# gMLP mixer of a macaron decoder step: squares of v added by transfers, mixing spread over three u chunks, first output product behind the fifth

## The chip, the cores and the metric

The kernel runs on one core of one Trainium2 chip. The metric is device time in microseconds (us), the median over runs of the same program. Everything is float32. Each large product is made of three TensorE products: operands are split into a high part (`_hi`, type float32r) and a rest (`_lo`), and hi·hi, lo·hi and hi·lo are added in PSUM.

## The reference

One step of a decoder trunk for 512 prompt tokens and 8 sample tokens (520 columns, TOK) with width 1024: per layer half a SwiGLU, a mixer, half a SwiGLU. The change lies in the mixer of layer 0, a gated MLP of inner width 2048:

```
def gmlp_mixer(h, w_in, b_in, v_gain, w_s, b_s, w_out):
    z = jax.nn.gelu(h @ w_in + b_in)
    u, v = z[..., :D_GMLP], z[..., D_GMLP:]
    v = rms_norm(v, v_gain)
    s = chunk_spatial_mix(v, w_s, b_s)   # per group g: (128x128 lower triangle of w_s[g]) @ v in blocks of 128 tokens, + b_s
    return (u * s) @ w_out, v
```

v needs its norm over all 2048 channels before anything can be mixed; u and the mixing go group by group (8 groups of 256 channels); for sample tokens the mixing is one factor and one bias per group.

## The kernel before, in words

Activations lie transposed: channels on the 128 partitions, the 520 tokens in the free dimension, `HALF` = 260 columns.

**Chunks.** `w_in` is worked through in 16 chunks of 256 columns: eight for v (v0 to v7 here), then eight for u (u0 to u7), then `w_out` in two output products of four chunks. A chunk of `w_in` is one `fast_chunk`: a Strassen-like scheme with seven blocks instead of eight (j = 0 to 6), each of 4 x 3 matmuls of 260 columns, so 84 matmuls. The blocks need sums of weight quarters (`sums_w`), and those take five engines:

- SP (SyncE) starts four loads per chunk (`load_fast`, L612, L616), two chunks ahead, when a `raw` slot is free.
- POOL (GpSimd) starts two transfers that add inside SBUF: `add_inner` (L3152, `sums_w<-raw`) when the loads have landed, `add_outer` (L3157, `raw<-raw`) when the first add has landed.
- DVE (VectorE) makes two more sums (`sums_second` L2207, `sums_last` L2214), the `_lo` rests of the weights (L2197), and takes the results out of PSUM (L2340, L2347, L2359, L2361, L2365: low0, high1, high0, both highs, low1).
- ACT (ScalarE) rounds weights to `w_hi` (L1492, L1496, L1501, L1516, L1518), copies three PSUM snapshots per chunk (L1573, L1579, L1589) and does Square and Gelu.
- PE (TensorE) runs the blocks (L842). Before block 6 it waits until DVE has taken high1 (L2347) out of the bank.

Every engine runs its own list in order and waits only on semaphores. Hooks (`between`, `steps`, `ready`, `mixing`, `own`, `held`, `behind`, `after`) put other work at set places of a chunk.

**Squares of v.** After each v chunk ACT squares its two channel tiles into `square` (L1477). POOL adds them into `square_sum` by two tensor instructions per chunk (`add_squares`, L3147; the first one is the copy L3144). The last pair is added during u0. Then PE sums over partitions (`rms_v`, L1025 to L1028, hook 5 of u0), ACT takes the root, DVE the reciprocal (`sample_gains`), and SP may load the biases `bs_all` into the tile `square` (L679; it waits for the finished sum, and SP's loads for u2 stand behind it in SP's list).

**Mixing.** For group g: PE transposes v (`turn_v`, L1041, L1042), ACT scales it into `v_tok` (L1920), PE multiplies by the mixing matrix (`mix`, L1053), DVE adds gain and bias into `tmp_mul` (L2772), POOL multiplies it with gelu(u) in `tmp_act` (L3222, two instructions of 128x520 per group), ACT copies to `hv`, DVE makes `h_lo` (L2784). Before, all of that for g stands in chunk u-g and the start of the next one. The first output product (`down`, L792) stands behind u3, the second behind u7.

## Time and profile before

| | |
|---|---|
| median of 3 runs | 2080.99 us (2080.2 to 2087.7) |
| the profiled execution's own time | 2089.98 us |
| its span in the profile | 2088.1 us |
| PE busy | 2042.7 us (98%) |
| DVE busy | 1677.0 us (80%) |
| ACT, POOL busy | 1170.7 us (56%), 372.2 us (18%) |
| granted TensorE clock | 0.998 of full |

The v chunks stand at about 374 to 466 us of the span, u0 to u3 at 466 to 526, the first output product at 528 to 574, u4 to u7 at 574 to 630, the second product from 632. The profile gives for every instruction its start and duration, and for idle time in front of it the instruction that ended it.

### The profile page before, as it was taken

How to read it: one execution, taken by the hardware profiler on the slowest of the kernel's cores; microseconds unless marked ns; L12 is line 12 of the kernel's file. 1: busy time of each engine (PE TensorE's matmuls, PEld its weight loads, DVE VectorE, ACT ScalarE, POOL GpSimd, SP SyncE). 2: the span in 40 equal slices, each digit the busy share in tenths (PEclk: the TensorE clock that was granted, in tenths of full speed). 3: DMA queues.
4: the chain of work that ended last, by engine and by line, in shares of the span. 5: the costliest groups of instructions: out<-in, count | busy, mean ns of one | idle time of the engine just before them, and what ended most of it. 6: DMA issues, size and time to landing. Idle time of an engine off the chain costs nothing.

```text
span 2088.1 us, 44481 instructions
## 1 busy us (share of the span) xinstructions
PE 2042.7 (98%) x16512; PEld 1972.9 (94%) x16512; DVE 1677.0 (80%) x2836; ACT 1170.7 (56%) x2101; POOL 372.2 (18%) x413
## 2 busy tenths in 40 slices
PE   9999999989999999999999999999999999999998
PEld 8999999988999999999999999998768889999998
DVE  6779887887477998998899998679665468989997
ACT  5446565666264655655665655445564346656555
POOL 0011111333131111110111111111122121111111
PEclk9999999999999999999999999999999999999999
DMA  5467775664445777775777777451322126777775
GB/s 160 123 162 179 181 184 149 148 152 122 112 112 128 175 179 176 181 186 151 168 177 181 178 186 181 129 138 28 96 72 81 61 61 158 179 184 176 187 181 128
DMA packets 385039, 307.52 MB, mean 147 GB/s; under 512 B 22951, under 2 KB 346836, under 8 KB 384628
## 3 DMA queue, kind: packets, MB, share of 16 engines
q1 hardware_dynamic: 343418, 231.03, 37.0%
q0 software_dynamic: 41152, 74.09, 21.9%
q8 instruction: 93, 1.52, 0.3%
q10 hardware_dynamic: 314, 0.37, 0.1%
q14 instruction: 62, 0.51, 0.1%
HBM read 228.76 MB, written 2.66 MB: 111 GB/s over the span
## 4 chain that ended last, share of the span: by engine, by line
PE 79%; DVE 6%; DMA 6%; issue 4%; ACT 2%; POOL 1%; SPq 1%; DVEq 0%; ACTq 0%; POOLq 0%
PE side L842 29%; PE main L842 20%; PE main L792 16%; DMA raw<-raw 2%; PE side L1389 2%; DVE w_lo L2197 2%; PE main L1151 2%; DMA sums_w<-raw 1%; DMA raw<-in_ffn_w_down 1%; PE main L1319 1%; PE side L1359 1%; POOL tmp_act L3222 1%; DMA raw<-in_ffn_w_gate 1%; PE side L1241 1%; PE main L1221 1%
## 5 line engine op out<-in xcount | busy, mean ns | idle before, releaser
L842 PE MATMUL side<-xw_hi,w_hi 128*128 128x260 f32 x1600 | 455.0, 284 | 20.1 <-DVE v L2347 9.2
L842 PE MATMUL side<-xw_hi,w_lo 128*128 128x260 f32 x1600 | 453.5, 283 | 0.0
L842 PE MATMUL side<-xw_lo,w_hi 128*128 128x260 f32 x1600 | 452.4, 283 | 0.0
L2197 DVE TENSOR_TENSOR w_lo<-raw,w_hi 128x512 fp32r<-128x512 f32 (+2 forms) x540 | 382.8, 709 | 71.0 <-ACT w_hi L1518 22.2
L842 PE MATMUL main<-xw_hi,w_hi 128*128 128x260 f32 x1200 | 341.5, 285 | 0.0
L842 PE MATMUL main<-xw_lo,w_hi 128*128 128x260 f32 x1200 | 338.9, 282 | 0.0
L842 PE MATMUL main<-xw_hi,w_lo 128*128 128x260 f32 x1200 | 338.7, 282 | 0.0
L842 PEld LDWEIGHTS side<-xw_hi,w_hi 128*128 128x128 f32 x1600 | 301.4, 188 | 25.6 <-DVE w_lo L2197 8.5
L842 PEld LDWEIGHTS side<-xw_hi,w_lo 128*128 128x128 f32 x1600 | 301.3, 188 | 0.0
L842 PEld LDWEIGHTS side<-xw_lo,w_hi 128*128 128x128 f32 x1600 | 301.0, 188 | 0.0
L2197 DVE TENSOR_TENSOR w_lo<-sums_w,w_hi 128x1024 fp32r<-128x1024 f32 (+2 forms) x264 | 250.3, 948 | 3.2 <-ACT w_hi L1501 3.2
L3152 POOL DMA_DIRECT2D sums_w<-raw x132 | 116.0, 879 | 756.0 <-DMA raw<-in_ffn_w_gate 321.9
L1516 ACT ACTIVATE w_hi<-raw 128x512 fp32r<-128x512 f32 (+1 forms) x132 | 83.2, 630 | 264.0 <-PE main L842 143.3
L842 PEld LDWEIGHTS main<-xw_hi,w_hi 128*128 128x128 f32 x1200 | 226.5, 189 | 0.2
L842 PEld LDWEIGHTS main<-xw_lo,w_hi 128*128 128x128 f32 x1200 | 226.2, 189 | 0.0
L842 PEld LDWEIGHTS main<-xw_hi,w_lo 128*128 128x128 f32 x1200 | 226.2, 189 | 0.0
L3157 POOL DMA_DIRECT2D raw<-raw x132 | 113.9, 863 | 399.6 <-DMA sums_w<-raw 399.6
L792 PE MATMUL main<-h_lo,w_hi 128*128 128x260 f32 x896 | 179.8, 282 | 0.0
L1496 ACT ACTIVATE w_hi<-raw 128x512 fp32r<-128x512 f32 (+1 forms) x264 | 164.2, 622 | 3.8 <-PE main L842 2.1
L1501 ACT ACTIVATE w_hi<-sums_w 128x1024 fp32r<-128x1024 f32 (+1 forms) x132 | 139.5, 1057 | 40.2 <-DVE sums_w L2207 38.2
L842 PE MATMUL side<-ht_hi,w_hi 128*128 128x260 f32 x496 | 140.9, 284 | 2.2 <-DVE tmp_in L2347 1.6
L842 PE MATMUL side<-ht_lo,w_hi 128*128 128x260 f32 x496 | 139.7, 282 | 0.0
(485 smaller groups left out, 4895.2 us busy)
## 6 DMA issues: line engine op xcount, KB each, us to landing
sums_w<-raw POOLq DMA_DIRECT2D x128, 256.0 KB, 3.3
raw<-raw POOLq DMA_DIRECT2D x128, 256.0 KB, 4.9
raw<-in_ffn_w_gate SPq DMA_DIRECT2D x86, 256.0 KB, 4.6
raw<-in_ffn_w_gate SPq DMA_DIRECT2D x43, 512.0 KB, 5.9
raw<-in_ffn_w_up SPq DMA_DIRECT2D x84, 256.0 KB, 4.7
raw<-in_ffn_w_up SPq DMA_DIRECT2D x42, 512.0 KB, 6.0
raw<-in_ffn_w_down SPq DMA_DIRECT2D x56, 256.0 KB, 4.4
raw<-in_ffn_w_down SPq DMA_DIRECT2D x28, 512.0 KB, 5.9
```

What stands on the lines that cost most here:

```text
L792: mm = nc.tensor.matmul(into[:, half, 0:HALF], w[:, k, m * P:(m + 1) * P], moving[:, k, half * HALF:(half + 1) * HALF], start=(k == 0 and ...
L842: mm = nc.tensor.matmul(into[j], w_tiles(w, weights_at(s, j))[:, k, :], moving[:, k, order[j], :], start=(j in (0, 1) and k == 0 and i == ...
L1151: mm = nc.tensor.matmul(main[:, u % 2, half, 0:HALF], st, moving[:, k, half * HALF:(half + 1) * HALF], start=(k == 0 and i == 0), stop=(k ...
L1221: mm = nc.tensor.matmul(main[:, h % 2, half, 0:HALF], wuk_t[:, h % 2, :], qn[:, h, half * HALF:(half + 1) * HALF], start=True, stop=True)
L1241: t_ = nc.tensor.transpose(side[:, bank, i * P:(i + 1) * P], pieces[2 * (first + i // 2) + half][:, j0 + i % 2, c0:c0 + P], ident)
L1389: mm = nc.tensor.matmul(side[:, 2, k * P:SEQ], rows[:, k, 0:KL], prob_t[:, PT_AT[k] * P:(PT_AT[k] + QB - k) * P], start=(k == 0), stop=(k ...
L1496: nc.scalar.activation(w_tiles(w_hi, j, nt), raw_odd(s, m, nt), ACT.Copy).then_inc(hi_done, 1)
L1501: nc.scalar.activation(w_pair(w_hi, nt), added_pair(s, nt), ACT.Copy).then_inc(hi_done, 1)
L1516: nc.scalar.activation(w_part(w_hi, 4, nt), raw_block(s, 1, nt), ACT.Copy)
L2197: a = nc.vector.tensor_tensor(dst, src, hi.bitcast(F32), ALU.subtract)
L3152: pool.dma_start(sums_w[:, 2 * s, 0:nt * P], raw_block(s, 1, nt), accum_op=ALU.add).then_inc(inner_added[s], 16)
L3157: pool.dma_start(raw_block(s, 1, nt), raw_block(s, 0, nt), accum_op=ALU.add).then_inc(outer_added[s], 16)
```

## The change

1. *Squares of v.* ACT writes the squares of v0 into `square_sum` and `tmp_mul`; those of v1 to v6 are added to these two tiles by two transfers per pair that POOL starts (`v_added`); DVE adds the pair of v7 and joins the chains (`v_sums`, in u0 where it made the sample gains before). ACT's Square moves from behind its second snapshot to behind its third. `rms_v` moves from hook 5 of u0 to the end of u0; the root moves behind u0, the reciprocals to the start of u1.
2. *Mixing.* The transposes for g stand at the end of u-g, `v_copies`, `mix` and DVE's mixing in the chunk behind it, `h_copies` and `rests` two chunks behind. gelu(u) is made in place, in `gm_in` and `tmp_act` by turns. The values for the sample tokens are made for all groups at once in `sm_all`; ACT, not DVE, fills `vs_tok`.
3. *Output.* The first output product stands behind u4 (U_FIRST = 5), the second behind u7 as before; `down` waits for the last four instead of the last two tiles one by one. POOL's list is reordered.

```diff
@@ SP: loads for u and out
+            for g in range(NG):
+                free = (l - 6, l - 5) if g not in (U_FIRST, U_FIRST + 1) else (l - 1, l - 1) if g == U_FIRST else (l - 5, l - 5)
+                load_fast(n % 2, w_in, g * WC, *free)
+                if g == 1:
+                    sp.wait_ge(sum_done, at_gmlp.sums + GT)
+                    sp.dma_start(bs_all, gmlp_b_s[0].partition_broadcast(P)).then_inc(bias_in, 16)
...
@@ PE
+            def first_turn():
+                rms_v()
+                turn_v(0)()
             for g in range(NG):
-                if g == 0:
-                    between = {5: rms_v, 6: turn_v(0, e - 4)}
-                elif g == 1:
-                    between = {1: mix(0), 3: turn_v(1, e - 4), 6: mix(1)}
-                else:
-                    between = {2: turn_v(g, e if g == NG // 2 else e - 4), 5: mix(g)}
+                between = {5: mix(g - 1), 7: turn_v(g)} if g else {7: first_turn}
+                if g == U_FIRST - 1:
+                    between.pop(7)
+                elif g == U_FIRST:
+                    between[2] = turn_v(g - 1, e)
+                elif g == NG - 1:
+                    between.update({6: turn_v(g), 7: mix(g)})
...
@@ ACT
             def v_squares(c):
                 def go():
-                    if c:
-                        act.wait_ge(sum_done, at_gmlp.sums + 2 * c)
                     act.wait_ge(act_done, at_gmlp.act + 2 * c + 2)
+                    if c == 0:
+                        nc.scalar.activation(square_sum[:], v[:, 0, :], ACT.Square).then_inc(square_done, 1)
+                        nc.scalar.activation(tmp_mul[:, 0, :], v[:, 1, :], ACT.Square).then_inc(square_done, 1)
+                        return
+                    if c >= 2:
+                        act.wait_ge(v_added[0], 16 * (c - 1))
+                        act.wait_ge(v_added[1], 16 * (c - 1))
                     nc.scalar.activation(square[:], v[:, 2 * c:2 * c + 2, :], ACT.Square).then_inc(square_done, 2)
...
-                steps = {2: v_squares(c - 1)}
+                steps = {"scales": v_squares(c - 1)}
...
                 if g == 0:
-                    steps = {2: v_squares(n_v - 1), 4: v_root}
+                    steps = {"scales": v_squares(n_v - 1)}
+                    after = [lambda: nc.scalar.activation(primed[:, 0:1], eps[:, 0:1], ACT.Sqrt), v_root]
                 elif g == 1:
-                    steps = {3: v_copies(1, (0, 1)), 4: h_copies(0)}
+                    steps = {"scales": v_copies(0), 4: u_gelu(0, e - 4)}
+                    after = [u_gelu(1, e)]
                 else:
-                    steps = {"turn": v_copies(g, (0,)), "scales": v_copies(g, (1,))}
-                    if g != NG // 2:
-                        steps[2] = h_copies(g - 1)
+                    steps = {"scales": v_copies(g - 1)}
+                    if g != U_FIRST:
+                        steps[1] = h_copies(g - 2)
+                    after = [u_gelu(g, e)]
+                if g == U_FIRST - 1:
+                    after = [h_copies(g - 1), u_gelu(g, e)]
+                elif g == NG - 1:
+                    after = [v_copies(g), u_gelu(g, e), h_copies(g - 1), h_copies(g)]
...
@@ DVE
+            def v_sums():
                 dve.wait_ge(square_done, at_gmlp.sums + GT)
                 vs = v[:, :, SEQ:TOK]
                 nc.vector.tensor_tensor(vs, vs, bc(v_gain, NS), ALU.mult).then_inc(vg_done, 1)
+                nc.vector.tensor_tensor(square[:, 0, :], square[:, 0, :], square[:, 1, :], ALU.add).then_inc(sum_done, 1)
+                for m in range(2):
+                    dve.wait_ge(v_added[m], 16 * (n_v - 2))
+                nc.vector.tensor_tensor(square_sum[:], square_sum[:], tmp_mul[:, 0, :], ALU.add).then_inc(sum_done, 1)
+                dve.wait_ge(sum_done, at_gmlp.sums + 2)
+                nc.vector.tensor_tensor(square_sum[:], square_sum[:], square[:, 0, :], ALU.add).then_inc(sum_done, GT - 2)
...
@@ POOL
             def add_v_squares(c):
-                for m in range(2):
-                    add_squares(m, at_gmlp.sums + 2 * c + m, c == 0 and m == 0)
+                pool.wait_ge(square_done, at_gmlp.sums + 2 * c + 2)
+                if c >= 2:
+                    for m in range(2):
+                        pool.wait_ge(v_added[m], 16 * (c - 1))
+                pool.dma_start(square_sum[:], square[:, 0, :], accum_op=ALU.add).then_inc(v_added[0], 16)
+                pool.dma_start(tmp_mul[:, 0, :], square[:, 1, :], accum_op=ALU.add).then_inc(v_added[1], 16)
...
             for c in range(n_v):
-                if c:
+                if c >= 2:
                     add_v_squares(c - 1)
                 add_chunk(c + 2)
-            add_v_squares(n_v - 1)
```

**POOL while v is made.** POOL's list from v1 on; `sums_w<-raw` and `raw<-raw` are the two weight adds of a chunk, `square_sum` collects the squares. Before:

```order
L3144 COPY square_sum<-square 128x520
L3147 TENSOR_TENSOR square_sum<-square_sum,square 128x520
L3152 DMA sums_w<-raw 128x512
L3157 DMA raw<-raw 128x512
L3147 TENSOR_TENSOR square_sum<-square_sum,square 128x520 x2
L3152 DMA sums_w<-raw 128x512
L3157 DMA raw<-raw 128x512
```

The same place in the changed kernel:

```order
L3261 DMA square_sum<-square 128x520
L3262 DMA tmp_mul<-square 128x520
L3199 DMA sums_w<-raw 128x512
L3204 DMA raw<-raw 128x512
L3261 DMA square_sum<-square 128x520
L3262 DMA tmp_mul<-square 128x520
L3199 DMA sums_w<-raw 128x512
```

The two tensor instructions of each chunk became two transfers at the same place, in front of the weight adds.

**DVE in u0.** DVE's list from high1 to low1 of u0, `gm_in` being the result of the chunk. Before:

```order
L2347 TENSOR_TENSOR gm_in<-root,side 128x260
L2197 TENSOR_TENSOR w_lo<-raw,w_hi 128x512
L2742 TENSOR_TENSOR v<-v,vectors 128x16x8
L2744 RECIPROCAL rv<-rv_root 128x12
L2745 RECIPROCAL rv<-rv_root 8x1
L2359 TENSOR_TENSOR gm_in<-main,root 128x260
```

In the changed kernel (high1 is now L2379, high0 L2391, the rests L2229):

```order
L2379 TENSOR_TENSOR gm_in<-root,side 128x260
L2229 TENSOR_TENSOR w_lo<-sums_w,w_hi 128x1024
L2229 TENSOR_TENSOR w_lo<-raw,w_hi 128x512
L2774 TENSOR_TENSOR v<-v,vectors 128x16x8
L2775 TENSOR_TENSOR square<-square 128x520
L2778 TENSOR_TENSOR square_sum<-square_sum,tmp_mul 128x520
L2780 TENSOR_TENSOR square_sum<-square_sum,square 128x520
L2391 TENSOR_TENSOR gm_in<-main,root 128x260
```

Three adds of 128x520 came in between high1 and high0, the wide rest moved from before high1 to behind it, and the reciprocals went to the start of u1.

**POOL in the u chunks.** POOL's list from u0 on, beginning with the weight adds for u2; `out<-vs_tok` is the output of the sample values, `tmp_act` the product. Before:

```order
L3152 DMA sums_w<-raw 128x512
L3157 DMA raw<-raw 128x512
L3216 DMA out<-vs_tok 8x256
L3222 TENSOR_TENSOR tmp_act<-tmp_act,tmp_mul 128x520 x2
L3152 DMA sums_w<-raw 128x512
L3157 DMA raw<-raw 128x512
L3216 DMA out<-vs_tok 8x256
L3222 TENSOR_TENSOR tmp_act<-tmp_act,tmp_mul 128x520 x2
```

In the changed kernel:

```order
L3199 DMA sums_w<-raw 128x512
L3204 DMA raw<-raw 128x512
L3199 DMA sums_w<-raw 128x512
L3204 DMA raw<-raw 128x512
L3267 DMA out<-vs_tok 8x256
L3274 TENSOR_TENSOR gm_in<-gm_in,tmp_mul 128x520 x2
L3199 DMA sums_w<-raw 128x512
L3204 DMA raw<-raw 128x512
L3267 DMA out<-vs_tok 8x256
L3274 TENSOR_TENSOR tmp_act<-tmp_act,tmp_mul 128x520 x2
```

Each of the first two multiplications now stands behind the weight adds of one chunk more.

## Rows read from the trace of the kernel before

**Rows 1.** Page, part 1: busy time, share of span, instructions.

```profile
PE 2042.7 (98%) x16512; PEld 1972.9 (94%) x16512; DVE 1677.0 (80%) x2836; ACT 1170.7 (56%) x2101; POOL 372.2 (18%) x413
```

**Rows 2.** Waits of PE, whole span: us in total, times, longest.

```profile
PE side L842 <- DVE v L2347: 9.2, 7, 1.7
PE side L842 <- ACT root L1589: 4.0, 5, 1.4
PE main L792 <- DVE gm_in L2359: 3.8, 2, 1.9
```

**Rows 3.** Windows: length; busy PE, PEld, DVE, ACT, POOL; clock, DMA share, GB/s.

```profile
395.75:466.10 70.35, 62.71 (x514) 61.56 (x514) 57.91 (x79) 43.50 (x73) 29.92 (x27) 1.00 0.67 161
466.10:528.00 61.90, 55.17 (x454) 53.28 (x453) 47.73 (x79) 38.77 (x84) 18.99 (x17) 1.00 0.42 113
574.50:631.70 57.20, 53.00 (x442) 51.92 (x441) 44.26 (x75) 34.59 (x79) 16.30 (x14) 1.00 0.41 109
```

**Rows 4.** Timeline of PE: start, us, instruction, [idle before]; two block-6 starts.

```profile
418.72 0.36 PE L842 MATMUL side<-xw_hi,w_hi 128*128 128x260 f32 x1 [1.23 <-DVE v L2347]
...
430.17 0.39 PE L842 MATMUL side<-xw_hi,w_hi 128*128 128x260 f32 x1 [1.17 <-DVE v L2347]
```

**Rows 5.** Timeline of DVE in the v chunk before 418.72.

```profile
413.66 1.39 DVE L2197 TENSOR_TENSOR w_lo<-raw,w_hi 128x512 fp32r<-128x512 f32 x1 [1.11 <-ACT w_hi L1492]
414.98 1.79 DVE L2214 TENSOR_TENSOR sums_w<-sums_w,raw 128x512 f32<-128x512 f32 x1
...
418.16 0.41 DVE L2347 TENSOR_TENSOR v<-root,side 128x260 f32 x1
...
419.55 0.70 DVE L2361 TENSOR_TENSOR v<-v,rstd_all 128x520 f32 x1
```

**Rows 6.** Timeline of POOL in the same chunk.

```profile
413.20 3.02 POOL L3147 TENSOR_TENSOR square_sum<-square_sum,square 128x520 f32<-128x520 f32 x2 [3.18 <-ACT square L1477]
417.01 0.88 POOL L3152 DMA_DIRECT2D sums_w<-raw  x1 [0.80 <-DMA raw<-in_gmlp_w_in]
420.63 0.88 POOL L3157 DMA_DIRECT2D raw<-raw  x1 [2.74 <-DMA sums_w<-raw]
```

**Rows 7.** Timeline of DVE in a later SwiGLU, the same kind of chunk.

```profile
740.64 0.43 DVE L2359 TENSOR_TENSOR th<-main,root 128x260 f32<-128x260 f32 x1 [0.31 <-PE main L842]
...
746.23 0.69 DVE L2197 TENSOR_TENSOR w_lo<-raw,w_hi 128x512 fp32r<-128x512 f32 x1
746.83 0.69 DVE L2214 TENSOR_TENSOR sums_w<-sums_w,raw 128x512 f32<-128x512 f32 x1
...
760.75 0.43 DVE L2359 TENSOR_TENSOR th<-main,root 128x260 f32<-128x260 f32 x1 [0.26 <-PE main L842]
```

**Rows 8.** Transfers issued or moved, 396 to 466 us.

```profile
q0 software_dynamic: 1872, 3.41, 28.9%
...
sums_w<-raw POOLq DMA_DIRECT2D x7, 256.0 KB, 3.3
```

**Rows 9.** Window of half a us with both queues at work.

```profile
430.00:430.50 0.50, 0.33 (x2) 0.33 (x3) 0.50 (x2) 0.19 (x1) 0.00 (x0) 1.00 1.12 197
```

**Rows 10.** Transfers, 656 to 686 us: squares added for a norm.

```profile
square_sum<-gm_in POOLq DMA_DIRECT2D x2, 260.0 KB, 4.9
```

**Rows 11.** Timeline of PE: a set of transposes, a mix, first output product.

```profile
500.04 0.66 PE L1041 MATMUL main<-const,v 128*128 128x128 f32 x4
...
507.13 1.05 PE L1053 MATMUL side<-ws_t,v_tok 128*128 128x128 f32 x8
...
528.06 0.48 PE L792 MATMUL main<-hv,w_hi 128*128 128x260 f32 x2 [1.92 <-DVE gm_in L2359]
```

**Rows 12.** Timeline of SP: the bias load.

```profile
473.75 0.34 SPq L679 DMA_DIRECT2D square<-in_gmlp_b_s  x1
```

**Rows 13.** Timeline of POOL: weight adds for u2.

```profile
481.24 0.88 POOL L3152 DMA_DIRECT2D sums_w<-raw  x1 [7.51 <-DMA raw<-in_gmlp_w_in]
...
486.58 0.86 POOL L3157 DMA_DIRECT2D raw<-raw  x1 [4.46 <-DMA sums_w<-raw]
```

182 lines of the change are left out of this document (97 added, 85 removed).

## The prediction

> **What bounds the kernel now.** I read the page's busy line first: PE is busy for 98% of the span [rows 1], so no change off PE can bring more than PE's idle time, 45 us. The list of waits says where that lies: the longest sums are waits for DVE's L2347 and ACT's L1589 before blocks of L842, and for L2359 before an output product [rows 2]. The windows put half of it into this mixer [rows 3]: PE is idle for 7.6 us of 70.35 in v2 to v7, 6.7 of 61.90 from u0 to the first product, 4.2 of 57.20 from u4 to the second. Elsewhere the change touches nothing, so the argument is on these three stretches.
>
> A stall costs more than its idle time. Two block-6 starts in the v chunks lie 11.45 us apart with 1.17 to 1.23 idle each [rows 4]; in a later SwiGLU the same chunk recurs every 20.11/2 = 10.05 us [rows 7]. So a v chunk loses 1.4 us, 0.2 more than the idle shows.
>
> Why DVE is late: beside POOL's two adds (3.02 us) its instruction L2197 took 1.39 and L2214 1.79 us [rows 5, 6]; without POOL's arithmetic both take 0.69 [rows 7]. That is 1.8 us of DVE per chunk, of which PE sees 1.4.
>
> **Part 1, the squares off POOL.** The six chunks v2 to v7 hold 70.35 us [rows 3]. At 10.05 each, with 0.8 for the one set of transposes of the mixing matrices in v2 (an estimate from the near-equal sets in [rows 11]), they hold 61.1. The most that can come back is 9.2 us.
>
> Against that stand two transfers of 260 KB per chunk. Price from below: the 14 weight adds in the v chunks took 28.9% of 70 us, 1.44 us of all 16 DMA engines each [rows 8], so a pair is 2.9 us. The DMA share is 0.67 [rows 3], 7.9 us per chunk; with the pair 10.8 us of DMA work in a chunk that should last 10.05, a share of 1.07. The trace shows half a microsecond at 1.12 [rows 9] (packets of two queues overlap a little), so it could just fit. Bounds: nothing (it fits), or 10.8 - 10.05 = 0.75 us per chunk, 4.5 us over six (share held at 1.0). What decides is when the inner weight add lands. Counted from a chunk's start, ACT's Square now ends near 5.9 and POOL issues the pair at 6 to 7.7; the loads for the next chunk land near 9 and the inner add goes into the queue behind the squares. It lands in 3.3 us when alone [rows 8]; squares added amid loads took 4.9 [rows 10]. That gives 12.7 to 14.5, 2.7 to 4.5 in the next chunk, and DVE can start L2207 as late as about 4.8 there without making PE wait (three instructions of 0.6, two of 0.35 and a wide rest of 1.2 before block 6 at 8.6). Near the edge, so I take 0.3 us per chunk, nearer to nothing than to the bound because the first chunks live on the lead that the loads have: 1.8 us. The v chunks bring 9.2 - 1.8 = 7.4 us.
>
> By the Trainium skill (DMA: Bandwidth & Descriptors, section on the anatomy of one GpSimd-issued DMA) such a transfer takes about 2.0 us plus its bytes at 436 GB/s, 2.6 us here, of which 0.6 moves data. By that the pair would load the engines for 1.2 us, the total would stay at 9.1 of 10.05, and the whole 9.2 us would come. The trace has 3.3 us for one and 1.44 of engine time, so it speaks against that reading.
>
> ACT's Square behind the third snapshot delays `sums_hi` by its 1 us and brings `first_hi` forward by as much; both wait for PE's blocks anyway. I put it at nothing; if the third snapshot's cover were gone it would cost up to 1 us per chunk, which is inside the bound of 0.75 that I keep. Writing two squares instead of copying (v0) costs ACT 0.2 us in v1, beside waiting.
>
> **Part 2, the turn from v to u.** DVE now makes the sum. In u0, block 4 ends 7.2 after the start; high1, a wide rest (1.2), a rest (0.6), the gains (0.2) and three adds of 0.7 [rows 5] follow in a row, to 11.8. PE has finished block 6 at 10.05 and waits: 1.8 us lost. Then come the sums over tokens and the transposes, about 2.5 us, so u1 starts at 14.3.
>
> SP's bias load waits for that sum: u0 + 11.8, where it was at 473.75, u0 + 7.65 [rows 12]. Behind it stand the loads for u2. From the bias load to the landing of u2's inner add it was 12.8 us [rows 12, 13]; the same again gives u0 + 24.6, u1 + 10.3. L2207, L2197, L2214, low0 and high1 then end at u1 + 12.8, where block 6 could start at 6 x 1.44 + 1.8 (mix) = 10.4: 2.4 us lost. Behind it DVE has the sample mixing for all groups (three small dependent instructions, under 1 us) and the two gain instructions, ACT has Gelu twice with a table load, and the snapshot for u2's block 2 is late: 1.3 us. Bounds for u0 and u1 together: from 1.8 (the weights land sooner) to 8 (they share the DMA engines with u3's loads and come 2 us later, all of it seen).
>
> **Part 3, the steady u chunks.** A mix is two sets of [rows 11], 1.8 us, a set of transposes twice about 0.55; a u chunk holds 13.0 us of PE work. The mixing inputs are a chunk old now, so ACT's L1589 waits should go: DVE's list is 10.2 us long, ACT's about 9.5, both under 13. Two places stay tight. POOL's second multiplication stands behind u4's weight adds, and ACT's `h_copies(1)` in u3 before the second snapshot waits for it: 1.1 us. In the two chunks that end in plain weights (u4, u7) DVE has a rest of 1.2 and two `rests` of 0.6 before low0, which come out 1.0 late at block 6; and L2359 still stands behind the two gain instructions. The first product waited 1.92 for it [rows 11]; without `vs_tok` in DVE's list 1.6. Behind u7 the last mix itself covers that wait, but the chain mix, gain, multiplication, copy, rest of the last tile then just reaches the product: 0.7. u5 and u6: 0.4 together.
>
> **The sum.** Before, the u stretches lose 6.7 + 4.2 idle [rows 3] and 0.2 for each of some 14 stalls, 13.7 us. After: 1.8 + 2.4 + 1.3 + 1.1 + (1.0 + 1.6) + 0.4 + (1.0 + 0.7) = 11.3. Gain 2.4; I take 2.1 for what POOL's multiplications slow on DVE. With 7.4 from v: 9.5 us. From the profiled execution's 2089.98 that is 2080.5. The median of the runs is 2080.99, 9 us under that execution, and the difference is no part of this mixer, so I carry it over: 2071.5 us.
>
> **Rivals.**
> *Everything hides.* The transfers fit between the loads (share 1.07 under 1.12) and the weights for u2 land before they are missed: 9.2 + 4 = 13.2, 2067.8. For it: the idle gaps in the DMA record of a v chunk. Against: rows 10.
> *The DMA engines bound the v chunks.* Period 10.8: 70.35 - 65.6 = 4.7 from v, 2.1 from u, 2074.2. For it: 10.8 us of work per chunk. Against: the 1.12.
> *Slower: the inner weight add waits behind the squares.* Both are in POOL's one queue. If each square takes its 4.9 us in turn, an inner add issued at 9.5 lands at 16 to 17 from the chunk's start, 6 to 7 in the next; L2207 is then 1.2 to 2.2 late, and each chunk lasts 11.3 to 12.3. From 11.6 on v gives a loss; at 12.0 it is 72.8 - 70.35 = 2.4 slower, and u with its upper bound adds nothing back (13.7 lost before, 15.5 after): 2085. For it: rows 10. Against: in rows 10 the loads were at work too, and the adds of a queue overlapped.
> *The change doesn't take the slowdown from DVE.* L2197 and L2214 could be slow because of the DMA traffic, not POOL. Rows 7 have the same traffic and 0.69 throughout, so I give it nothing of its own.
>
> **Chances.** Forecast (2069 to 2074) 0.48, everything hides 0.22, DMA bound 0.17, slower 0.13. What a measurement of this kernel can tell from no change is 0.5%, 10.4 us: faster is below 2070.6, slower above 2091.4. Faster takes the second case whole and 0.21 of the first; slower keeps 0.05, the tail of the last. The likeliest case alone is 2069 to 2074; the range that leaves 2 in 10 out goes from 2063 to 2083.
>
> **What would show it.** In the profile after: L2197 and L2214 at 0.69 in all v chunks; block-6 starts 10.05 to 10.6 apart (10.8: DMA bound; over 11.6: the queue); the DMA share in v near 1.0; PE idle once for 1.8 before the token sums; L2207 in u1 near u1 + 10 with PE idle 2 to 3 us at block 6; ACT waiting for POOL in u3; the wait of 1.6 before the first product kept, that before the second gone. I am wrong if L2207 waits for `sums_w<-raw` in every v chunk, or if the u stretches lose more than 13.7.

## The result and the profile after

The changed kernel is 0.4% slower: 2092.66 us (median of 12 runs, 2089.72 to 2095.7) against 2085.78 for the kernel before (12 runs beside it, 2080.2 to 2089.59), ratio 1.0037 with a 95% interval of 1.0028 to 1.0046. The forecast was 9.5 us faster; the kernel became 6.9 us slower.

The page's busy line of the profile after:

```profile
PE 2046.0 (98%) x16512; PEld 1977.2 (95%) x16512; DVE 1667.4 (80%) x2826; ACT 1169.3 (56%) x2111; POOL 356.4 (17%) x409
```

POOL lost 16 us of arithmetic and DVE 10, as meant [rows 1]; PE is 3.3 us busier with as many matmuls. To see where the time went I measure positions from one instruction, PE's first matmul of the sums over tokens ahead of the mixer: 378.53 before, 374.42 after (this profile ran 4.1 us ahead there, in work that the change doesn't touch). From it I take the start of DVE's L2365 (after: L2397) in v7, the last remainder of that chunk, the starts of the two output products, and the token sums of the next layer:

| us | last v chunk | from there to product 1 | product 1 to product 2 | to the next layer | sum |
|---|---|---|---|---|---|
| before | 87.95 | 61.58 | 103.66 | 53.70 | 306.89 |
| after | 86.16 | 79.55 | 94.47 | 53.60 | 313.78 |

The sum is 6.9 us longer, as much as the medians differ. The agreement to a tenth is chance: outside these marks the two profiled executions differ too, by 4.1 us ahead of them and about 1.6 behind them. (A u chunk moved from behind product 1 to ahead of it, so its two columns are read together: 165.24 before, 174.02 after.) The v chunks brought 1.8 us where 7.4 were forecast, the u chunks lost 8.8 where 2.1 were to be gained.

The waits of PE over the whole span, after (total, times, longest), beside [rows 2]:

```profile
PE side L846 <- ACT main L1591: 9.5, 9, 1.8
PE main L1048 <- DVE tmp_mul L2815: 3.7, 1, 3.7
PE side L846 <- DVE tmp_act L2379: 2.8, 1, 2.8
PE main L1048 <- issue: 2.0, 1, 2.0
...
PE side L846 <- DVE v L2379: 1.6, 1, 1.6
```

L846, L1591 and L2379 are the L842, L1573 (ACT's first snapshot) and L2347 of before. The wait for DVE in the v chunks fell from 9.2 us to 1.6; ACT's first snapshot, on which PE hardly waited, took its place, and four single waits are new (3.7, 2.8, 2.0 and 1.6).

**The v chunks after.** The transfers moved between 392 and 462 us: queues, and medians from issue to landing, beside [rows 8]:

```profile
q0 software_dynamic: 3262, 5.98, 47.3%
q1 hardware_dynamic: 12672, 7.87, 39.8%
...
square_sum<-square POOLq DMA_DIRECT2D x6, 260.0 KB, 6.9
tmp_mul<-square POOLq DMA_DIRECT2D x6, 260.0 KB, 7.6
raw<-raw POOLq DMA_DIRECT2D x6, 256.0 KB, 7.0
...
sums_w<-raw POOLq DMA_DIRECT2D x6, 256.0 KB, 6.7
```

An inner addition of weights that took 3.3 us takes 6.7. Timelines of POOL, ACT, DVE and PE in one v chunk show what hangs on it:

```profile
411.09 0.86 POOL L3199 DMA_DIRECT2D sums_w<-raw  x1 [0.49 <-DMA raw<-in_gmlp_w_in]
419.53 0.86 POOL L3204 DMA_DIRECT2D raw<-raw  x1 [7.58 <-DMA sums_w<-raw]
420.43 0.86 POOL L3261 DMA_DIRECT2D square_sum<-square  x1
```

```profile
426.73 0.63 ACT L1534 ACTIVATE w_hi<-raw 128x512 fp32r<-128x512 f32 x1 [5.06 <-DMA raw<-raw]
...
427.79 1.33 ACT L1896 ACTIVATE v<-v,vectors 128x520 f32<-128x520 f32 x2
429.02 0.37 ACT L1591 ACTIVATE main<-side 128x260 f32<-128x260 f32 x1
```

```profile
419.36 0.69 DVE L2239 TENSOR_TENSOR sums_w<-sums_w,raw 128x512 f32<-128x512 f32 x1 [1.09 <-DMA sums_w<-raw]
419.96 0.68 DVE L2229 TENSOR_TENSOR w_lo<-raw,w_hi 128x512 fp32r<-128x512 f32 x1
420.57 0.68 DVE L2246 TENSOR_TENSOR sums_w<-sums_w,raw 128x512 f32<-128x512 f32 x1
```

```profile
429.44 0.39 PE L846 MATMUL side<-xw_hi,w_hi 128*128 128x260 f32 x1 [1.75 <-ACT main L1591]
```

L2229 and L2246 are at 0.69 where L2197 and L2214 took 1.39 and 1.79 [rows 5], as forecast. But the outer addition can be issued only when the inner has landed, for which POOL now waits 7.58 us (2.74 before, [rows 6]). It lands after 426, ACT sits 5.06 us in front of its high part (3.97 to 5.06 in five of the chunks), then come the gate's Gelu and the snapshot, and PE waits 1.75. The loss is not the same in every chunk: from one high1 to the next it takes 10.61, 10.46, 11.97, 13.16, 11.18 and 11.26 us, where before it took 12.89 once and then 11.49 to 11.55. I had followed the inner addition to DVE, where it came 1.09 late and PE saw none of it, and not the outer to ACT.

**The windows after**, v2 to v7 and 1.3 us more, then from v7 to product 1 (columns as in [rows 3]):

```profile
391.70:461.90 70.20, 65.84 (x528) 64.79 (x527) 47.95 (x79) 41.77 (x72) 20.85 (x24) 0.98 0.87 199
...
460.60:540.10 79.50, 68.52 (x535) 66.43 (x534) 55.64 (x89) 46.41 (x102) 17.35 (x18) 0.94 0.48 118
```

The u stretch has lost twice: 11 us idle, and a granted TensorE clock of 0.94 (1.00 before).

**The chunk u1 after**, on SP, POOL, DVE and PE, beside [rows 12, 13]:

```profile
473.52 0.34 SPq L681 DMA_DIRECT2D square<-in_gmlp_b_s  x1
473.90 0.43 SPq L615 DMA_DIRECT2D raw<-in_gmlp_w_in  x1
```

```profile
482.60 0.86 POOL L3199 DMA_DIRECT2D sums_w<-raw  x1 [15.80 <-DMA raw<-in_gmlp_w_in]
488.58 0.86 POOL L3204 DMA_DIRECT2D raw<-raw  x1 [5.12 <-DMA sums_w<-raw]
...
495.32 2.85 POOL L3274 TENSOR_TENSOR gm_in<-gm_in,tmp_mul 128x520 f32<-128x520 f32 x2
```

```profile
488.32 0.69 DVE L2239 TENSOR_TENSOR sums_w<-sums_w,raw 128x512 f32<-128x512 f32 x1 [7.42 <-DMA sums_w<-raw]
...
495.37 3.38 DVE L2393 TENSOR_TENSOR tmp_act<-tmp_act,rstd_all 128x520 f32<-128x520 f32 x1
```

```profile
473.54 1.05 PE L1031 MATMUL side<-const,square_sum 128*128 128x1 f32 x8 [1.64 <-DVE square_sum L2780]
...
491.04 0.36 PE L846 MATMUL side<-xw_hi,w_hi 128*128 128x260 f32 x1 [2.79 <-DVE tmp_act L2379]
...
495.10 1.09 PE L1048 MATMUL main<-const,v 128*128 128x128 f32 x4 [1.98 <-issue]
...
515.23 0.39 PE L846 MATMUL side<-xw_hi,w_hi 128*128 128x260 f32 x1 [1.20 <-ACT main L1591]
```

The bias rows go into the tile `square`, so their load waits for the last sum, at 473.5; the loads of u2's weights stand behind it. POOL waits 15.8 us for them, DVE 7.4, PE 2.8. What followed was not in the forecast: the mixing is behind on DVE, so the next turn waits 1.98 (it is not issued before DVE has mixed the pair before); POOL's multiplication starts together with L2393, which takes 3.38 us for its usual 0.70, and again in u2 (3.53, at 509.99) and behind product 1 (3.39, at 599.06); ACT's Gelu and snapshot are late by that, and PE waits 1.20 in u3. And windows of the same profile:

```profile
473.50:478.00 4.50, 4.46 (x27) 4.25 (x28) 2.72 (x7) 0.41 (x2) 0.00 (x0) 0.67 0.64 174
...
491.00:495.00 4.00, 2.08 (x12) 1.81 (x12) 3.90 (x9) 3.32 (x5) 0.77 (x2) 0.63 0.50 85
495.00:498.00 3.00, 2.90 (x14) 2.76 (x15) 2.97 (x3) 0.00 (x0) 3.00 (x4) 0.50 0.56 96
```

Behind these waits the windows show a granted clock of 0.50 to 0.67 (0.50 is the lower of its two levels, 1.2 of 2.4 GHz), and the four transposes at 495.10 take 1.09 us for 0.66 [rows 11].

### The profile page after: what moved, and what is told of

It reads as the page before. It is cut to its first block, busy times and chain, and to the rows that moved or that the text cites. A ratio compares the mean times of both kernels' runs of the same rounds, so it can differ in the third digit from the quotient of the medians.

```text
span 2089.3 us, 44439 instructions
## 1 busy us (share of the span) xinstructions
PE 2046.0 (98%) x16512; PEld 1977.2 (95%) x16512; DVE 1667.4 (80%) x2826; ACT 1169.3 (56%) x2111; POOL 356.4 (17%) x409
## 4 chain that ended last, share of the span: by engine, by line
PE 77%; DMA 9%; DVE 6%; issue 3%; ACT 3%; SPq 1%; POOL 0%; DVEq 0%; ACTq 0%; POOLq 0%
PE side L846 27%; PE main L846 20%; PE main L796 16%; DMA raw<-raw 4%; DMA sums_w<-raw 2%; PE side L1402 2%; DVE w_lo L2229 2%; PE main L1164 2%; DMA raw<-in_gmlp_w_in 1%; DMA raw<-in_ffn_w_down 1%; PE main L1332 1%; PE side L1372 1%; DMA raw<-in_ffn_w_up 1%; DMA raw<-in_ffn_w_gate 1%; PE side L1254 1%
## 5 line engine op out<-in xcount | busy, mean ns | idle before, releaser
L846 PE MATMUL side<-xw_hi,w_hi 128*128 128x260 f32 x1600 | 456.2, 285 | 17.6 <-ACT main L1591 9.5
L846 PE MATMUL side<-xw_hi,w_lo 128*128 128x260 f32 x1600 | 454.7, 284 | 0.0
L846 PE MATMUL side<-xw_lo,w_hi 128*128 128x260 f32 x1600 | 453.6, 283 | 0.0
L2229 DVE TENSOR_TENSOR w_lo<-raw,w_hi 128x512 fp32r<-128x512 f32 (+2 forms) x540 | 374.6, 694 | 70.5 <-ACT w_hi L1536 29.2
L846 PE MATMUL main<-xw_hi,w_hi 128*128 128x260 f32 x1200 | 341.9, 285 | 0.0
L846 PE MATMUL main<-xw_lo,w_hi 128*128 128x260 f32 x1200 | 339.4, 283 | 0.0
L846 PE MATMUL main<-xw_hi,w_lo 128*128 128x260 f32 x1200 | 339.3, 283 | 0.0
L846 PEld LDWEIGHTS side<-xw_hi,w_hi 128*128 128x128 f32 x1600 | 302.9, 189 | 22.8 <-ACT main L1591 11.7
L846 PEld LDWEIGHTS side<-xw_hi,w_lo 128*128 128x128 f32 x1600 | 302.5, 189 | 0.0
L846 PEld LDWEIGHTS side<-xw_lo,w_hi 128*128 128x128 f32 x1600 | 302.4, 189 | 0.0
L2229 DVE TENSOR_TENSOR w_lo<-sums_w,w_hi 128x1024 fp32r<-128x1024 f32 (+2 forms) x264 | 249.4, 945 | 3.3 <-ACT w_hi L1519 3.2
L846 PEld LDWEIGHTS main<-xw_hi,w_hi 128*128 128x128 f32 x1200 | 227.1, 189 | 0.2
L846 PEld LDWEIGHTS main<-xw_lo,w_hi 128*128 128x128 f32 x1200 | 226.8, 189 | 0.0
L846 PEld LDWEIGHTS main<-xw_hi,w_lo 128*128 128x128 f32 x1200 | 226.8, 189 | 0.0
L846 PE MATMUL side<-ht_hi,w_hi 128*128 128x260 f32 x496 | 140.8, 284 | 1.3 <-DVE tmp_in L2379 0.6
L846 PE MATMUL side<-ht_lo,w_hi 128*128 128x260 f32 x496 | 139.7, 282 | 0.0
```

What stands on the lines that cost most here:

```text
L846: mm = nc.tensor.matmul(into[j], w_tiles(w, weights_at(s, j))[:, k, :], moving[:, k, order[j], :], start=(j in (0, 1) and k == 0 and i == ...
L2229: a = nc.vector.tensor_tensor(dst, src, hi.bitcast(F32), ALU.subtract)
```

## Experiments

All positions are those of the table above, each from one profiled execution. How far such a number can be trusted is seen from kernels with the same v code: with the change's transfers 84.65, 84.89, 85.43, 86.16 and 86.98 (five executions of four kernels), with POOL's arithmetic 82.23, 82.28, 82.28 and 82.33 (four). For the stretch from v7 to product 1 two executions of one kernel gave 71.05 and 69.66. Differences under about 2 us are told only where several kernels share them. A ratio is to the kernel before, timed beside it. The expectations of e1 and e2 put the changed kernel's v stretch at 87.7; its trace has 86.16.

| kernel | last v | to product 1 | to product 2 | sum | ratio |
|---|---|---|---|---|---|
| e1, no squares added | 78.99 | 79.08 | 94.06 | 305.74 | 0.9994 (0.9981 to 1.0006) |
| e2, transfers last | 83.97 | 77.57 | 94.85 | 310.00 | 1.0026 (1.0015 to 1.0037) |
| e3, transfers between | 82.58 | 78.74 | 94.76 | 309.68 | |
| e4, Square two steps earlier | 85.02 | 79.58 | 94.77 | 312.93 | |
| e12, one transfer a pair | 81.18 | 79.52 | 94.76 | 309.07 | |
| e5, bias load later | 84.89 | 71.05 | 93.16 | 302.70 | |
| e13, the same, timed | 85.43 | 69.66 | 94.34 | 303.04 | 0.9979 (0.9964 to 0.9993) |
| e6, last turn later | 84.65 | 79.34 | 93.10 | 310.60 | |
| e7, multiplication later | 86.98 | 76.26 | 93.17 | 309.98 | |
| e8, POOL adds squares | 82.33 | 74.36 | 93.09 | 303.38 | 0.9998 (0.9986 to 1.0010) |
| e9, before, Square later | 82.28 | 60.84 | 104.62 | 301.42 | 0.9966 (0.9954 to 0.9978) |
| e14, e8 and bias load later | 82.23 | 66.05 | 94.27 | 296.10 | 0.9961 (0.9944 to 0.9978) |
| e10, e14 and multiplication later | 82.28 | 66.24 | 93.10 | 295.23 | 0.9951 (0.9935 to 0.9967) |
| e11, e3, bias load and multiplication later | 84.23 | 71.29 | 93.14 | 302.22 | 0.9975 (0.9962 to 0.9989) |

### What the transfers of squares cost (e1 to e4, e12)

**e1** issues none of them, so the squares of v1 to v6 are missing from the sum.

```diff
-                if c >= 2:
-                    add_v_squares(c - 1)
                 add_chunk(c + 2)
```

> The changed kernel without the twelve transfers that add squares of v1 to v6 (their share is missing from the norm of v; all else as it was). Lengths are counted from the token sums of v0 to DVE's last instruction on v (low1 of v7): 87.95 us in the kernel before, 87.7 in the changed one. Theory Q (the square transfers stand ahead of the weight adds in POOL's queue and make them late): both costs of the squares are gone, so block-6 starts come 10.05 us apart and the stretch is 78 to 80 us. Theory D (the DMA engines are the bound): the same. Theory A (ACT's Square behind the third snapshot is what makes ACT late): stays near 87. The u stretches as in the changed kernel, +7 us over before.

The v chunks end at 78.99, from v3 on 10.10 us each, as theories Q and D both said (78 to 80); PE is never idle between 395 and 454. So the most that v could bring was 87.95 - 78.99 = 9.0 us (forecast 9.2), and the transfers cost 86.16 - 78.99 = 7.2 us (5.7 to 8.0 over the five executions), not 1.8. The whole is 6.5 us under the changed kernel in the median, 8.0 in the sum and 9 by the two ratios, and 7.2 of it lie in v: the u chunks are as slow as with the transfers (79.08 for 79.55), so their loss does not come from these.

**e2** puts the squares by turns into two tiles and issues their transfers behind both weight additions; **e3** puts them between the inner and the outer addition.

```diff
+                add_inner(c % 2, at_gmlp.wsum + 2 * (c + 2))
                 if c >= 2:
                     add_v_squares(c - 1)
-                add_chunk(c + 2)
+                add_outer(c % 2, at_gmlp.wsum + 2 * (c + 2))
```

> The changed kernel with the square transfers of a pair put behind both weight adds in POOL's list, and Square writing by turns into two tiles so that ACT needn't wait for them. Same bytes moved. Theory Q: weight adds land in 3.3 to 4 us again, the v stretch falls from 87.7 to 79 to 81 us and the kernel gains 7 to 8 us against the changed one (about the time of before). Theory D: the transfers take the same engine time wherever they stand, the period stays above 11 us and the stretch above 85. Theory A: no change.

> As the run with the squares last, but with them between the inner and the outer weight add. Theory Q: the inner add lands in 3.3 to 4 us, only the outer one is late by up to 3 us; ACT, which waits for the outer add before Gelu, stalls for less than 4 to 5 us a chunk but still stalls; the v stretch is 80 to 85 us. Theory D: above 85, like the order of the changed kernel.

Last v chunk at 83.97 and 82.58; e2 lies between what Q (79 to 81) and D (above 85) said, e3 where Q said. Another place in POOL's queue gives back 0.4 to 4.4 us, by which executions one compares. Of the cost 3.6 to 5.2 us stay in these two orders (e11 below, with the order of e3, ended v at 84.23). POOL's timeline in e2 and then in e3:

```profile
440.42 0.86 POOL L3204 DMA_DIRECT2D raw<-raw  x1 [6.41 <-DMA sums_w<-raw]
```

```profile
451.65 0.86 POOL L3204 DMA_DIRECT2D raw<-raw  x1 [1.07 <-DMA sums_w<-raw]
```

In e2 the squares of the same round stand behind this addition, and still the inner addition took over 6 us: those of the round before are under way. In e3 the inner addition stands ahead of its round's squares, which POOL issues right behind it, and lands in 3.42 us.

**e4** moves ACT's Square back to its old place (`steps = {2: v_squares(c - 1)}`).

> The changed kernel with ACT's Square back behind the second snapshot, as before; transfers and their order unchanged. Theory A: the v stretch falls to 80 to 82 us. Theory Q: the pair is issued about 1.4 us earlier, ahead of the weight adds by more, so the weight adds may come up to 1.4 us sooner: 83 to 88 us, ACT still stalls before the outer add in most chunks.

Last v chunk at 85.02, within the scatter of the changed kernel's own: with transfers the Square's place is worth nothing that one execution can show.

**e12** leaves out one of the two transfers of each pair (the odd squares of v1 to v6 are not in the sum).

> The changed kernel with one of the two transfers of squares of each pair left out, so that the odd squares of the pairs v1 to v6 are missing from the sum. Theory D (a transfer costs by the bytes that the DMA engines move beside the additions of weights): the last v chunk lies about half way, at 81.5 to 84 us after the token sums (79.0 with none, 84.7 to 87.0 with two), and an outer addition of weights lands 4.5 to 6 us after its issue (3.3 with none, 7.0 with two). Theory Q (the price is the place in POOL's queue ahead of the additions of weights, and one transfer takes as good as the same place): 84 us or more.

81.18, a little under what theory D expected. The price rises with what is moved: 0, 2.2 and 5.7 to 8.0 us for no, one and two transfers, for the second more than for the first; but one transfer less is also less ahead in POOL's queue, and e12's 2.2 us are a single long chunk. An outer addition lands in 5.5 us, as theory D said, but in e1, without any transfer of squares, it takes 5.5 too and not the 3.3 of that expectation, so this tells nothing. Over the v chunks the medians from issue to landing are, for the inner addition, 3.3 in e1, 4.5 in e12, 6.7 in the changed kernel and 7.0 in e2, where squares are under way ahead of it, but 3.9 in e3 and 3.7 in e11, where as a rule they only follow it; for the outer 5.5 in e1 and e12, 7.0 in the changed kernel, 6.7 in e2, 6.8 in e3 and 6.1 in e11. So what stands ahead in the queue is what delays the inner addition (theory Q), while the outer one of the changed kernel, with nothing ahead of it and the squares behind, takes 7.0 for 5.5, which speaks for the load (theory D). How the 7.2 us divide between the two stays open: in every order one of a chunk's two additions meets the squares, and no run puts these into another queue.

### The place of ACT's Square with POOL's arithmetic (e8, e9)

**e8** is the changed kernel with POOL's old additions in place of the transfers; ACT's Square stays where the change put it.

```diff
-                pool.dma_start(square_sum[:], square[:, 0, :], accum_op=ALU.add).then_inc(v_added[0], 16)
-                pool.dma_start(tmp_mul[:, 0, :], square[:, 1, :], accum_op=ALU.add).then_inc(v_added[1], 16)
+                for m in range(2):
+                    add_squares(m, at_gmlp.sums + 2 * c + m, c == 0 and m == 0)
```

> The squares of v are added by POOL's arithmetic as in the kernel before, the u chunks are those of the change. Theory D with Q (the transfers' price is nearly the whole of POOL's arithmetic, and the u chunks lose on their own): last v chunk at 87 to 89 us after the token sums (86.2 changed, 88.0 before), from there to the end of the second output product 224 to 228 us (227.6 changed, 218.9 before), so that the whole is 5 to 9 us above the kernel before. Rival (the u chunks lose because the backlog of the squares' transfers and the late sum reach into them, not by their own order): from the last v chunk to the end 219 to 222 us, and the whole within 3 us of the kernel before.

Theory D with Q missed in both stretches, and the rival gave the right numbers for the second: 221.05 us from v7 to the end, the whole 1.4 us under before in the median (by the ratio, not told from it). What it says of u is half true: e1, without transfers but with DVE's sum at the end of u0, took 79.08 to product 1, and e8, with the sum on POOL, 74.36. It is the late sum that reaches into u, not the backlog. Neither foresaw v: its chunks end at 82.33, 5.6 us ahead of before, from v2 on at 10.3 us each, with the very arithmetic that was to be blamed. The one edit left in v is the one that I had priced at nothing. **e9** makes it alone, in the kernel before:

```diff
-                steps = {2: v_squares(c - 1)}
+                steps = {"scales": v_squares(c - 1)}
```

> The kernel before with one edit: ACT's Square of a v pair stands behind the scaled stripes of the next chunk (as in the changed kernel) instead of two steps ahead of them. POOL's arithmetic, POOL's order and the u chunks are those of before. Theory P (it is this move that takes POOL's additions away from the two DVE instructions between a chunk's second and third block; with them gone the v chunks run at 10.3 us each, as they did with POOL's arithmetic in the changed kernel, for 11.5): last v chunk 82 to 83 us after the token sums for 88.0, the whole 4 to 6 us shorter than before, ratio 0.997 to 0.998. Rival (the short chunks seen there need the changed u part or were that one execution's): periods of 11.0 to 11.5 us and the whole within 1.5 us of before. Second rival (v gains, but the last squares, and so the sums, come no earlier and the u chunks give it back): the last v chunk 5 us earlier and the end within 2 us.

82.28, as theory P said, and 0.34% off the whole, by one line. POOL and DVE in a v chunk of e9:

```profile
432.07 3.56 POOL L3147 TENSOR_TENSOR square_sum<-square_sum,square 128x520 f32<-128x520 f32 x2 [2.31 <-ACT square L1477]
```

```profile
431.04 0.69 DVE L2214 TENSOR_TENSOR sums_w<-sums_w,raw 128x512 f32<-128x512 f32 x1
432.21 0.43 DVE L2340 TENSOR_TENSOR v<-main,rstd_all 128x260 f32 x1 [0.48 <-PE main L842]
432.97 1.49 DVE L2197 TENSOR_TENSOR w_lo<-sums_w,w_hi 128x1024 fp32r<-128x1024 f32 x1 [0.33 <-ACT w_hi L1501]
434.38 0.41 DVE L2347 TENSOR_TENSOR v<-root,side 128x260 f32 x1
434.72 1.46 DVE L2197 TENSOR_TENSOR w_lo<-raw,w_hi 128x512 fp32r<-128x512 f32 x1
```

POOL's additions still slow DVE, but other instructions of it: the splits around L2347 take 1.49 us for 1.21 and 1.46 for 0.69, 1.0 in all, and L2197 and L2214 ahead of L2340, which lost 1.8 [rows 5], run at 0.69. What is lost now lies behind or beside the instruction for which PE waited, and POOL takes 3.56 us for 3.02 [rows 6]. In its list of waits the 9.2 us for L2347 [rows 2] have become 3.2, in the whole span:

```profile
PE side L842 <- DVE v L2347: 3.2, 2, 1.6
```

One of these two waits, in v1, is no matter of POOL: e1 and the changed kernel have it too (1.60). The other is in v2, where POOL's additions still meet L2214 and L2197 (2.36 and 2.00 us). From v1 to v2 it takes 12.80 us there, 2.3 more than in e1, which is most of the 3.3 us by which v ends later with POOL's arithmetic than without any addition.

The one line does a second thing. Before, DVE's L2197 waited 1.11 us for ACT's high part L1492 [rows 5], which stood right behind the Square in ACT's list:

```profile
412.05 1.07 ACT L1477 ACTIVATE square<-v 128x1040 f32<-128x1040 f32 x1
413.01 0.62 ACT L1492 ACTIVATE w_hi<-raw 128x512 fp32r<-128x512 f32 x1
```

In e9 it stands ahead of the Square, and DVE waits no longer. So before, DVE came 1.1 + 1.8 = 2.9 us late, of which PE saw 1.2. The wait for ACT alone costs PE nothing: e4 has the Square at its old place and no arithmetic on POOL, and in a v chunk with the same wait (L1510 is its L1492) DVE is still ahead of PE, which is not idle:

```profile
399.22 0.69 DVE L2229 TENSOR_TENSOR w_lo<-raw,w_hi 128x512 fp32r<-128x512 f32 x1 [1.11 <-ACT w_hi L1510]
401.20 0.43 DVE L2372 TENSOR_TENSOR v<-main,rstd_all 128x260 f32 x1 [0.68 <-PE main L846]
```

What POOL's 1.8 us alone would cost no run shows. My estimate from these figures is next to nothing, 1.8 less the 2.9 - 1.2 = 1.7 us that DVE has to spare: PE was held because both came together.

### The u chunks (e5 to e7, e13)

**e5** and **e13** are one kernel: the bias load behind the loads of u2 (`if g == 2:` for `if g == 1:` ahead of it). What these expectations call the weights of u1 are the weights of u2, which are summed and split during u1.

> The load of the bias rows, which waits for the squares' sum, stands behind the loads of u2 on SP instead of ahead of them; nothing else differs from the changed kernel. Theory S (u1's weights are late because their loads stood behind the bias load, which waits for the last sum): PE's wait of 2.8 us for DVE's remainder in u1 falls under 1 us, the first output product starts 2 to 3 us earlier after the token sums (165.7 in the changed kernel, 163 to 164 here), the whole 2 to 3 us shorter. Rival (the weights are late because the additions of weights are behind the backlog of the squares' transfers, and the first output product is held by the mixing's turns anyway): the wait moves to a later instruction of u1 or u2 and the product starts within 0.7 us of where it did.

> The same kernel as the run with the bias load behind u2's loads, now timed over three rounds. Theory S (this load's place costs the changed kernel 8 to 10 us, 5 of them waits of PE and 3 the TensorE clock at its lower level behind them): ratio to the kernel before 0.998 to 1.0, that is 8 to 11 us below the changed kernel's 1.0037. Rival (that execution was a lucky one and the load costs about the 2.4 us of the one wait): ratio 1.002 to 1.003.

From v7 to product 1 it takes 71.05 and 69.66 for 79.55, three times what theory S of e5 had asked for, and the ratio falls from 1.0037 to 0.9979, as theory S of e13 said: 12 us for one index by the ratios, 9.5 by the medians. PE in u0 to u4 of e5:

```profile
472.41 1.05 PE L1031 MATMUL side<-const,square_sum 128*128 128x1 f32 x8 [1.64 <-DVE square_sum L2780]
488.98 0.63 PE L1048 MATMUL main<-const,v 128*128 128x128 f32 x4 [0.55 <-issue]
```

The waits of 2.79, 1.98 and 1.20 are 0, 0.55 and 0. In the window that answers to 460.60:540.10 the same matmuls keep PE busy for less:

```profile
459.50:530.60 71.10, 65.64 (x536) 64.47 (x535) 54.04 (x89) 46.61 (x102) 17.88 (x18) 0.98 0.53 133
```

65.64 for 68.52 with the granted clock at 0.98 for 0.94: 2.9 us of the 8.4 are the clock, 5.4 the three waits. L2393 takes 0.97 in u1, though POOL's multiplication is still at work; that started 0.9 us ahead of it and not together with it (e13):

```profile
490.50 3.02 POOL L3274 TENSOR_TENSOR gm_in<-gm_in,tmp_mul 128x520 f32<-128x520 f32 x2 [0.60 <-DVE tmp_mul L2815]
```

```profile
491.38 0.97 DVE L2393 TENSOR_TENSOR tmp_act<-tmp_act,rstd_all 128x520 f32<-128x520 f32 x1
```

**e6** moves PE's turn of u7 to the chunk's end (`between[7]` for `between[6]`, ahead of the last mix).

> In u7 PE's turn of the last pair stands at the end of the chunk, just ahead of the mixing matmuls, instead of one block earlier; nothing else differs from the changed kernel. Theory T (the turn waits for DVE's mixing of the pair before, 3.7 us in u7, and PE has a block of other work that it could do in that time): the wait falls under 2 us and the second output product starts 1.5 to 3 us earlier (260.2 after the token sums in the changed kernel), and the last four remainders still come before their matmuls, so that the end (313.8) moves as much. Rival (the chain turn, copy, mixing, multiplication, copy, remainder of the last pair bounds the output product): the product starts earlier but waits at its twelfth to sixteenth tile, and the end stays within 0.5 us or is later.

The wait of 3.67 is gone and three others have come, for the turn, DVE and the copies (0.80, 1.02, 1.23). Product 1 to product 2 takes 93.10; the kernels that kept the wait took 93.09 to 93.17 (e5, e7, e8, e10, e11) or 94.06 to 94.85 (all others with the changed u part). So it gains 1.7 us at most and perhaps nothing: the waits of the last pair's chain took the place of the one removed.

**e7** lets POOL's multiplication wait until DVE has run L2393.

```diff
+                if g < NG - 1:
+                    pool.wait_ge(row_set, at_gmlp.rows + n_v + g + 2)
                 for m in range(2):
```

> POOL's multiplication of a pair waits until DVE has written the high parts of the next chunk's last block, so that the two do not run side by side; nothing else differs from the changed kernel. Theory M (side by side with POOL's multiplication DVE's instruction on two SBUF inputs takes 3.4 us for 0.7, and this holds up Gelu and ACT's snapshot, on which PE waits): these instructions take 0.7 in u1 to u4, PE's waits of 1.2 and 0.9 us for the snapshot go, and the first output product starts 1.5 to 3 us earlier (165.7 in the changed kernel). Rival: PE is held by the turns, which wait for the mixing and so for the multiplication before it; a later multiplication makes these waits longer, and the product starts at 165.5 or later.

L2393 takes 0.70 in all four chunks, and v7 to product 1 falls from 79.55 to 76.26, as theory M said; the turn's wait grew from 1.98 to 2.4, as the rival said, by less (one execution). Whether this is a loss of its own, e14 tells.

### Together (e10, e11, e14)

> The changed kernel with POOL's arithmetic for the squares, the bias load behind the loads of u2, and POOL's multiplication behind the next chunk's high parts. If the three effects found apart add up (v stretch 82.3; from the last v chunk to the second output product 167.5 with POOL's squares, of which the late weights of u1 3 and the collision 3): the second output product at 243 to 245 us and the end at 297 to 299 us after the token sums (before 306.9, changed 313.8), the whole 5 to 9 us below the kernel before, ratio 0.996 to 0.9975. Rival (both fixes remove waits ahead of the same turn, so that only the larger counts): end at 300 to 302, ratio 0.998 to 1.0.

> The changed kernel with its transfers kept, in two buffers and issued between the inner and the outer addition of weights, the bias load behind the loads of u2, and POOL's multiplication behind the next chunk's high parts. Theory D (the transfers hold up the additions of weights for as long as they are there): last v chunk at 82 to 84 us as in the run with that order, second output product at 243 to 247, end at 297 to 301 us, ratio 0.996 to 0.999, no faster than with POOL's arithmetic. Rival (the transfers are the better way once nothing stands behind them): last v chunk under 81 us and the end 2 us or more ahead of the kernel with POOL's arithmetic.

> The changed kernel with POOL's arithmetic for the squares and the bias load behind u2's loads; the multiplication stands where the change has it. Theory M (the collision of the multiplication with DVE's high parts costs on its own, some 3 us): from the last v chunk to the first output product 68 to 70 us (66.2 with the multiplication moved as well, 74.4 with neither), the whole about 3 us above that kernel, ratio 0.9960 to 0.9975. Rival (the collision only follows from the late weights, and where these come in time the two instructions miss each other or the wait is hidden): 66 to 67 us, ratio 0.9945 to 0.996.

e14 and e10 differ by e7's edit alone and take 66.05 and 66.24 to product 1: once the weights come in time, it is worth nothing there, so theory M falls and the collision was a consequence of the late weights. The trace of e14 has the instruction of the collision at 0.70 in u1 and u2 and 0.97 in u3, where e8, with the late weights, has 3.29, 3.86 and 0.97. (e10's sum is 0.9 us shorter, all of it behind product 1; the intervals of the two ratios overlap.) e10's sum and ratio are better than its expectation, which let the effects add up; e11's v stretch and sum end 0.2 and 1.2 us behind what theory D gave it, and its rival falls. e10 against e11 is the price of the transfers, in the order of e3, with everything else mended: 295.23 for 302.22, a ratio of 0.9951 for 0.9975. 2 us of it are in the v chunks and 5 between v7 and product 1, where DVE's sum holds PE for 1.63 us and the sums over tokens start 11.6 us after v7 for 9.3. From v7 to product 2 e10 takes 159.34 us for the 165.24 of before: the spreading of the mixing does bring time. e10 has the lowest time of all, though it is not told from e14: 2075.15 us for 2087.39, 0.5% faster than before and 0.9% faster than the changed kernel by the two ratios. PE's waits of over 0.3 us in it from 404 us to product 1 are these:

```profile
481.60 0.63 PE L1048 MATMUL main<-const,v 128*128 128x128 f32 x4 [0.51 <-issue]
520.80 0.36 PE L846 MATMUL side<-xw_hi,w_hi 128*128 128x260 f32 x1 [1.02 <-DVE gm_in L2374]
523.67 0.48 PE L796 MATMUL main<-hv,w_hi 128*128 128x260 f32 x2 [1.20 <-DVE gm_in L2386]
```

## Why the prediction was wrong

**Right.** The ceiling of v, 9.2 us (9.0). The instructions L2197 and L2214 at 0.69 and POOL as their cause. PE's wait for the sum in u0, 1.8 (1.64); for DVE's remainder in u1, 2.4 (2.79); the remainder in u4, 1.0 (1.02), and the wait ahead of product 1, 1.6 (1.21). The wait ahead of product 2 is gone, but PE waits 3.67 for a transpose 6 us ahead of it. One reading was off: the three windows hold 18.6 of PE's 45 us of idle time, not half.

**The step that failed in v** is "Near the edge, so I take 0.3 us per chunk". Measured: 1.2 (7.2 over the six, in chunks of 10.1 to 13.7 us). Three things were wrong in it. It chose the value near the lower bound on the strength of half a microsecond at a share of 1.12 [rows 9]; over a whole stretch the transfers held 0.87, and an addition landed in 6.7 to 7.0 us where I had allowed the inner one 3.3 to 4.9. It placed what decides at the inner addition and DVE's L2207, but each pair of additions is a chain of two landings, and the outer's reader is ACT, with Gelu and a snapshot behind it. And its upper bound, 0.75 a chunk by the engines' work alone, left out that chain, so the truth lay outside. The rival "slower: the inner weight add waits behind the squares" had part of the mechanism at the wrong price: it followed the delay to DVE alone, at 11.3 to 12.3 us a chunk, and let v lose from 11.6 on. Its time, 2085, was the nearest of all, and that is luck: it had v 2.4 us slower, which came 1.8 faster, and u 1.8 slower, which came 8.8 slower (its 15.5 for u doesn't come out of my bounds either, which give 11.3 - 5.5 + 8 = 13.8).

**The step that failed in the moved Square** is "I put it at nothing". Alone it is worth 5.7 us, most of what v had to give, and the change could have had it without one transfer. I priced the move on ACT and by its own microsecond. What it moves is the start of what waits for it: POOL's 3 us of arithmetic, and with it the place where DVE is slow, and ACT's high part behind it, for which DVE waited 1.11. The trace of before held what was needed: POOL's additions started when ACT's Square ended, and [rows 5, 6] show which two DVE instructions they met, and the wait of 1.11 in front of the first. "POOL's arithmetic makes DVE late" was therefore only a part of the reason for the 1.4 us a chunk.

**The step that failed in u** is "2.4 us lost", "1.3 us" behind it. The first wait was right, and what hung on it was not followed: the turn's own wait for DVE's mixing (1.98), the multiplication now beside L2393, the snapshot (1.20), and 2.9 us of clock, for which the sum had no term. The bias load's place cost 8.5 to 9.9 us in positions (e5, e13), 9.5 in the medians and 12 by the ratios, for 3.7 in the sum. DVE's sum in place of POOL's was priced at PE's wait, 1.8; with the bias load mended it costs 3.6 to 5.0 from v7 to product 1 (e5 and e13 against e14), since everything of the mixing starts behind it. In u7 the turn waits 3.67 for the mixing before; my sum had 0.7 for the chain behind it. The forecast wait of 1.1 for POOL in u3 came as 1.20 for ACT's first snapshot, by the collision and not by the queue I had named; that number was luck. From v7 to product 2 the kernels line up: 165.24 before, 174.02 changed, 164.21 and 164.00 with the bias load mended (e5, e13), 160.32 with POOL's arithmetic as well (e14). With both mended u brings 4.9 us, so the steady chunks were not overrated.

**The carried difference.** Before's profiled execution was 9 us over the median of its three first runs; over 12 runs the median is 2085.78. Of the 21 us between forecast and result 5 come from this.

By the Trainium skill (SBUF — State Buffer, section on who interferes with whom) a DVE instruction with two inputs in SBUF contends with a GpSimd instruction that reads SBUF. The trace agrees for L2393 (0.70 alone, 3.38 started together with POOL's multiplication, 3.16 to 3.86 in e1 and e8 within 0.4 us of its start), and the page names the rule that I should have laid over the moved instructions as well as over the removed ones. How much it costs depends here on who starts when: 0.97 where DVE started 0.9 us later.

## What to carry to other kernels

- When an instruction is moved, price what waits for it and what stands behind it in its list, on every engine: a move that costs its own engine nothing can shift another engine's slow stretch onto or off the critical instruction, and two delays that are each hidden can hold the critical engine together. Try the move alone before the rewrite that contains it.
- A load whose wait ends late stops every load behind it in its queue; list what stands behind a waiting issue before anything else. Here one index was worth some 10 us of 2090.
- Here DMA engines at a share of 0.67 had no room for two more transfers a chunk beside additions that come in chains of two landings: count the landings up to the last reader, and take the price of a transfer from a stretch as busy as the one it will create.
